# A fused mixer, MoE and two attention layers: split fills that run 8 chunks ahead, with their low parts kept in the weight ring

## The reference

```python
def even_layer(x, mem, ...):
    h = rms_norm(x, g) @ w_in
    y = concat([gdn_branch(...), diff_attention(dq, dk, dv, dg, ...), memory_attention(mq, mg, mem, ...)])
    return x + y @ w_out

def diff_attention(q, k, v, gate, ...):          # 8 heads, two softmaxes each
    q, k = rms_norm(q), rms_norm(k)
    p = softmax(q1 @ k1.T * scale + bias) - lam * softmax(q2 @ k2.T * scale + bias)
    return rms_norm(p @ v) * (1 - lambda_init) * silu(gate)

def odd_layer(x, mem, positions, ...):
    h = rms_norm(x, g) @ w_in                     # sq sk sv sg | mla q | c_kv | k_rope | mla gate | mq mg
    y = concat([window_attention(...), mla_attention(...), memory_attention(...)])
    return x + y @ w_out

def mla_attention(q, c_kv, k_rope, gate, positions, ...):
    k_nope, v = split(rms_norm(c_kv) @ w_kv_up)
    k = rms_norm(concat([k_nope, broadcast(k_rope)])); q = rms_norm(q)
    q, k = rope(q, positions), rope(k, positions)
    return softmax(q @ k.T * scale) @ v * silu(gate)
```

## Time and profile before

| | |
|---|---|
| median of 3 runs | 2868.59 us (2864.26 to 2870.82) |
| profiled execution | 2862.06 us, span 2860.3 us |
| mean granted clock of TensorE | 0.966 of full |
| PE busy | 2573.9 us, 90% of the span |
| DVE, ACT, POOL busy | 1334.4, 1087.0, 511.7 us |
| fill chunks | 288 (lows L798 x288, mean 1395 ns) |

### The profile page before, as it was taken

The page is one execution under the profiler, slowest core; times in us unless marked ns, Lnnn a source line. Parts: engine busy times, 40 slices in busy tenths (PEclk is TensorE's granted clock), DMA queues, the critical chain, the costliest instruction groups (busy, mean ns, idle before and its releaser), DMA issues. The chain is left out here.

```text
span 2860.3 us, 39591 instructions
## 1 busy us (share of the span) xinstructions
PE 2573.9 (90%) x14740; PEld 1873.2 (65%) x14740; DVE 1334.4 (47%) x2501; ACT 1087.0 (38%) x1922; POOL 511.7 (18%) x411
## 2 busy tenths in 40 slices
PE   8999999998888889999989999677889988978888
PEld 7984556886544444459957768565678767756667
DVE  5654784664211112347745545533435433474443
ACT  5553122443222122235434224344445344434444
POOL 0000110020011100010000000555530065064332
PEclk9999999999999999999999999898899989999999
DMA  7754344553599999945420135322244533432332
GB/s 300 220 205 152 134 145 144 184 199 123 239 422 422 422 421 422 380 187 179 172 81 32 46 126 197 119 103 103 103 148 150 177 114 115 147 118 104 130 116 107
DMA packets 80320, 529.77 MB, mean 185 GB/s; under 512 B 9088, under 2 KB 13568, under 8 KB 18848
## 3 DMA queue, kind: packets, MB, share of 16 engines
q1 hardware_dynamic: 76128, 514.50, 47.5%
q0 software_dynamic: 3456, 11.02, 1.5%
q10 hardware_dynamic: 576, 2.10, 0.2%
HBM read 520.24 MB, written 7.34 MB: 184 GB/s over the span
## 5 line engine op out<-in xcount | busy, mean ns | idle before, releaser
L798 POOL TENSOR_TENSOR parts_wl<-ring,parts_wh 128x512 fp32r<-128x512 f32 x288 | 396.3, 1395 | 1160.8 <-ACT parts_wh L783 1156.0
L759 PE MATMUL ps<-parts_wh,layer_xh 128*128 128x512 f32 x576 | 251.6, 437 | 107.8 <-POOL parts_wl L798 45.1
L2302 PE MATMUL ps<-ring,yT 128*64 128x256 f32 x2048 | 247.7, 386 | 52.6 <-DMA ring<-in_weights 48.5
L783 ACT ACTIVATE parts_wh<-ring 128x512 fp32r<-128x512 f32 x288 | 175.9, 629 | 276.9 <-PE ps L761 260.5
L760 PE MATMUL ps<-parts_wl,layer_xh 128*128 128x512 f32 x576 | 240.1, 417 | 0.0
L761 PE MATMUL ps<-parts_wh,layer_xl 128*128 128x512 f32 x576 | 239.6, 416 | 0.0
L2302 PEld LDWEIGHTS ps<-ring,yT 128*64 128x64 f32 x2048 | 137.7, 137 | 155.6 <-DMA ring<-in_weights 91.2
L1169 PE MATMUL ps<-ring,xT 128*128 128x512 f32 x512 | 222.0, 592 | 2.8 <-PEq L488 1.7
L759 PEld LDWEIGHTS ps<-parts_wh,layer_xh 128*128 128x128 f32 x576 | 117.3, 204 | 149.4 <-issue 58.6
L413 DVE TENSOR_TENSOR split_wl<-ring,split_wh 128x512 fp32r<-128x512 f32 x208 | 145.3, 709 | 96.5 <-ACT split_wh L387 95.4
L456 ACT ACTIVATE features_wh<-ring 128x512 fp32r<-128x512 f32 x208 | 130.3, 631 | 133.3 <-PE ps L473 133.3
(11 more groups left out here) (671 smaller groups left out, 5328.9 us busy)
## 6 DMA issues: line engine op xcount, KB each, us to landing
ring<-in_weights SPq DMA_DIRECT2D x468, 1024.0 KB, 5.0
x_res<-in_x SPq DMA_DIRECT2D x1, 2048.0 KB, 7.6
yT<-in_mem SPq DMA_DIRECT2D x1, 2048.0 KB, 15.7
rel_skew<-lru_feat POOLq DMA_DIRECT2D x1, 2048.0 KB, 49.8
mem_features<-yT ACTq DMA_DIRECT2D x4, 512.0 KB, 6.9
s_wb<-in_s_bc POOLq DMA_DIRECT2D x4, 512.0 KB, 3.9
s_wc<-in_s_bc POOLq DMA_DIRECT2D x4, 512.0 KB, 3.9
gate_bias<-in_gate_bias POOLq DMA_DIRECT2D x8, 256.0 KB, 3.9
```

What stands on the lines that cost most here:

```text
L759: mm(out, xh[:, kc, at], wh[:, c, :], start=kc == 0, stop=False)
L783: k.nc.scalar.activation(k.parts[0][:, c, :], k.ring[:, slot, c * BLK:(c + 1) * BLK], ACT.Copy).then_inc(w_high.sem, 1)
L798: k.nc.gpsimd.tensor_tensor(k.parts[1][:, c, :], k.ring[:, slot, c * BLK:(c + 1) * BLK], k.parts[0][:, c, :], ALU.subtract)\
L2302: last = nc.tensor.matmul(k.ps[s * WIN:(s + 1) * WIN, p, 0:FF], window[:, p, kc, :], k.ring[:, slot, at:at + FF], start=kc == 0, stop=kc = ...
```

## The change

- `LATE_DEEP = 8`: eight high buffers in place of four, and the lows lead by eight.
- The low part is written over the raw weights in the ring slot (`w_low` has the ring's address), so a slot is freed only by PE's last use of its low parts, in `gemm_tokens(late=True)` too.
- Steps are given out anew, so that blocks mostly end where a slot ends. In the attention, DVE stores an ended block after it has mixed the probabilities, not before.
- All four blocks of the latent input are fills of the window attention; the gate is cut into two blocks, one there, one in the MLA fill. The `gemm_tokens` at the start of `mla_branch` is gone.
- The rotary key's product is split like the others (`KeyProduct`): POOL makes high and low parts during the window gemm, and PE multiplies beside the norm of the latent.
- In `mla_rope`, ACT makes the two sines first and then the highs; evictions come once, at the end.

```diff
+LATE_DEEP = 8
...
-    CREDIT = SPLIT_DEEP
+    CREDIT = LATE_DEEP
...
 def gemm_tokens(...)
+        def high(j, kc):
+            return k.w_high[:, (j * chunks + kc) % deep, :] if late else wh[:, kc % deep, :]
+
+        def low(unit, turn, j, kc):
+            c = kc % UNIT_KC
+            return k.w_low[:, slot_of(unit, turn, 2 * upb), c * BLK:(c + 1) * BLK] if late else wl[:, kc % deep, :]
...
+                            if late and c == UNIT_KC - 1:
+                                mid.then_inc(k.unit_used, 1)
...
-                        dve.drain().then_inc(k.unit_used, 1)
+                        if not late:
+                            dve.drain().then_inc(k.unit_used, 1)
...
 class SplitFill:
-    LEAD = SPLIT_DEEP
+    LEAD = LATE_DEEP
...
-            act.wait_ge(w_used.sem, w_used.at(step - SPLIT_DEEP))
+            act.wait_ge(w_used.sem, w_used.at(step - self.LEAD))
...
+class KeyProduct:
+    def split(self, pool):
+        k, high = self.k, self.k.ev("small_high")
+        pool.wait_ge(k.loaded, k.loads)
+        k.nc.gpsimd.tensor_copy(self.high[:, :, :], self.raw).then_inc(high.sem, 1)
+        pool.wait_ge(high.sem, high.at(0))
+        k.nc.gpsimd.tensor_tensor(self.low[:, :, :], self.raw, self.high[:, :, :], ALU.subtract)
+    def multiply(self, pe, steps):
...
+            for kc in range(KC):
+                mm(out, xh[:, kc, at], self.high[:, kc, :], start=kc == 0, stop=False)
+                mm(out, xh[:, kc, at], self.low[:, kc, :], start=False, stop=False)
+                last = mm(out, xl[:, kc, at], self.high[:, kc, :], start=False, stop=kc == KC - 1)
...
 def attention(...)            # DVE
                     store(0)
                     if more:
                         begin(i + 1)
-                    store(1)
                     for j in pair:
...
                             dve.drain().then_inc(mixed.sem, 1)
-                    store(2)
+                    store(i, 1)
+                    store(i, 2)
...
-MEM_STEPS = {"evm": (8, (5, 5, 4, 2), 8), "odm": (6, (3, 3, 2, 2), 6)}
...
-              fill=fill, steps=first)
+              fill=fill, steps=8)
...
-              fill=fill, steps=steps)
+              fill=fill, steps=(3, 3, 1, 1))
...
-    head_norm(k, [v[:, t, 0:n].rearrange("p (h w) -> p h w", w=64) for v in (pq, pd) for t in range(NT)], 64, free, fill=fill, steps=8)
+    head_norm(k, [v[:, t, 0:n].rearrange("p (h w) -> p h w", w=64) for v in (pq, pd) for t in range(NT)], 64, free, fill=fill, steps=24)
...
-              fill=fill, steps=(5, 4, 4, 3), turned=free.rearrange("p (j a) -> p j a", j=2))
+              fill=fill, steps=[(4, 4, 4, 4)] * 3 + [(3, 3, 1, 1)], turned=free.rearrange("p (j a) -> p j a", j=2))
...
-              turn=Turned(k, lambda c, t: pq[:, t, c * P:(c + 1) * P], diff_x, HEADS, 7))
+              post=1.0 - lambda_init, gate=[pd[:, t, 2 * n:3 * n] for t in range(NT)], fill=fill, steps=16, early=8,
+              turn=Turned(k, lambda c, t: pq[:, t, c * P:(c + 1) * P], diff_x, HEADS, 14))
...
-        fill = SplitFill(k, (k.layer, KC, 2, tokens_to(k, mla_gate), None), (k.layer, KC, 2, tokens_to(k, pq), None))
+        fill = SplitFill(k, (k.layer, KC, 4, tokens_to(k, pq), None), (k.layer, KC, 1, tokens_to(k, mla_gate), None))
...
-        wait_loads(k, reach, bias, fill=fill, steps=4)
+        wait_loads(k, reach, bias, fill=fill, steps=8)
...
-        gemm_tokens(k, None, 2, KC // UNIT_KC, *store_tokens(k, pq, 2 * BLK), whole=k.layer, parts=k.parts)
...
-            rms_scale(k, ckv, ckv, n=KV_RANK, squares=squares)
+            rms_scale(k, ckv, ckv, n=KV_RANK, squares=squares, fill=product)
...
-            mla_rope(k, inner, pos, q_parts, kr, kv, rstd, free, fill, (8, 6))
+            mla_rope(k, inner, pos, q_parts, kr, kv, rstd, free, fill, 16)
...
+        k.w_high = nc.alloc_sbuf_tensor_at("late_wh", [P, LATE_DEEP, BLK], F32R, offset=xT_at)
+        k.w_low = nc.alloc_sbuf_tensor_at("late_wl", [P, LATE_RING, UNIT_KC * BLK], F32R, offset=ring_at)
```

More of the change, by code:

```diff
@@ L298, in first_pieces, with gemm_tokens @@
     return [slice(0, 1), slice(1, UNIT_KC)] + [slice(g, g + UNIT_KC) for g in range(UNIT_KC, chunks, UNIT_KC)]
-def gemm_tokens(k, x, blocks, upb, finish_act, finish_dve, dve_after_act=False, ahead=None, deep=SPLIT_DEEP, beside=None, after=None,
-                into=None, whole=None, parts=None, product=None):
+def gemm_tokens(k, x, blocks, upb, finish_act, finish_dve, dve_after_act=False, ahead=None, beside=None, after=None,
+                into=None, whole=None, late=False):
     nc, base = k.nc, k.used
@@ L386, in body @@
                             act.wait_ge(w_used.sem, w_used.at(j * chunks + kc - deep, turn, per))
-                            nc.scalar.activation(wh[:, c % deep, :], raw(unit, turn, c), ACT.Copy).then_inc(w_high.sem, 1)
+                            nc.scalar.activation(high(j, kc), raw(unit, turn, c), ACT.Copy).then_inc(w_high.sem, 1)
                         if g == 0 and not first:
@@ L412, in body @@
                             dve.wait_ge(w_high.sem, w_high.at(j * chunks + kc, turn, per))
-                            last = nc.vector.tensor_tensor(wl[:, c % deep, :], raw(unit, turn, c), wh[:, c % deep, :], ALU.subtract)
-                            last.then_inc(w_low.sem, 1)
-                        dve.drain().then_inc(k.unit_used, 1)
+                            nc.vector.tensor_tensor(low(unit, turn, j, kc), raw(unit, turn, c), high(j, kc), ALU.subtract).then_inc(w_low.sem, 1)
+                        if not late:
+                            dve.drain().then_inc(k.unit_used, 1)
                         if g == 0 and not first:
@@ L426, in gemm_tokens @@
     k.ended(evac_a=blocks, evac_v=blocks, x_high=len(pieces), x_low=len(pieces), w_high=steps, w_low=steps, w_used=steps)
-    if product is not None:
-        product.end()
 class FeatureSplit:
@@ L782, in make_highs @@
             slot, c = unit_wait(k, act, self.base + step // UNIT_KC, 0, 0), step % UNIT_KC
-            k.nc.scalar.activation(k.parts[0][:, c, :], k.ring[:, slot, c * BLK:(c + 1) * BLK], ACT.Copy).then_inc(w_high.sem, 1)
+            k.nc.scalar.activation(k.w_high[:, step % self.LEAD, :], k.ring[:, slot, c * BLK:(c + 1) * BLK], ACT.Copy).then_inc(w_high.sem, 1)
             self.high_at = step + 1
@@ L797, in lows @@
             pool.wait_ge(w_high.sem, w_high.at(step))
-            k.nc.gpsimd.tensor_tensor(k.parts[1][:, c, :], k.ring[:, slot, c * BLK:(c + 1) * BLK], k.parts[0][:, c, :], ALU.subtract)\
+            at = slice(c * BLK, (c + 1) * BLK)
+            k.nc.gpsimd.tensor_tensor(k.w_low[:, slot, at], k.ring[:, slot, at], k.w_high[:, step % self.LEAD, :], ALU.subtract)\
                 .then_inc(w_low.sem, 1)
@@ L2620, in end, with head_norm @@
         self.k.ended(turn_ready=1, tr=self.groups, **({"turn_high": self.groups} if isinstance(self.dst, tuple) else {}))
-def head_norm(k, parts, width, scratch, eps=EPS, mean=True, gain=None, post=1.0, gate=None, fill=None, steps=0, turn=None):
+def head_norm(k, parts, width, scratch, eps=EPS, mean=True, gain=None, post=1.0, gate=None, fill=None, steps=0, turn=None, early=0):
     nc = k.nc
@@ L2655, in _ @@
                     at += n
+                if early:
+                    fill.store_dve(dve, early)
                 if gain is not None:
@@ L2666, in _ @@
                     dve.drain().then_inc(k.ev("turn_ready").sem, 1)
-                    fill.store_dve(dve, turn.first)
+                    fill.store_dve(dve, turn.first - early)
                     turn.evict_dve(dve)
@@ L2670, in _ @@
                 elif fill:
-                    fill.store_dve(dve, steps)
+                    fill.store_dve(dve, steps - early)
             @block.gpsimd
@@ L2687, in _ @@
                     act.drain().then_inc(gated.sem, 1)
+                if early:
+                    fill.store_act(act, early)
                 if turn:
-                    fill.store_act(act, turn.first)
+                    fill.store_act(act, turn.first - early)
                     turn.evict_act(act)
@@ L2692, in _ @@
                 elif fill:
-                    fill.store_act(act, steps)
+                    fill.store_act(act, steps - early)
             @block.tensor
@@ L2809, in _ @@
                 if fill:
-                    fill.load(sp, turns * sum(steps))
+                    fill.load(sp, sum(sum(s) for s in by_turn))
             @block.gpsimd
@@ L2814, in _ @@
                 for i in range(turns if fill else 0):
-                    fill.lows(pool, sum(steps))
+                    fill.lows(pool, sum(by_turn[i]))
                     if beside is not None:
@@ L4139, in _ @@
             load(k, sp, pos[:, :], k.dram["positions"])
-            fill.load(sp, sum(steps))
+            fill.load(sp, steps)
         @block.tensor
         def _(pe):
-            fill.multiply(pe, sum(steps))
+            fill.multiply(pe, steps)
         @block.vector
@@ L4211, in _ @@
```

(2 more changed lines are left out.)

153 lines of the change are left out of this document (72 added, 81 removed).

## The result

The changed kernel takes 2838.98 us (median of 4 runs, 2836.61 to 2840.72) where the kernel before, on the same chip, takes 2866.43: a ratio of 0.9904, 95% interval 0.9885 to 0.9924. It is 27 us faster; 59 were forecast. Measured again later it stood at 0.9924 (0.9907 to 0.9941). The profiled execution took 2840.7 us, its span 2839.0.

What follows compares the result with a forecast made beforehand. TensorE was taken as the bound, at work 90% of the span, the end being its matmuls plus its holes. Stage terms summed to about -59 us on the profiled 2862.1: 2803, or 2810 in the runs; 8-in-10 range 2784 to 2848.

Steps and rivals of the forecast that it cites:

- Diff head norm: First stretch, 24 chunks instead of 8: 30.3 to 61 us, +31, with PE stalled about 12.6 us at chunk 17.
- both other head norms: Window head norm, 23.7 to 33.5 us (+9.8), and MLA head norm, 24.4 to 38.3 us (+13.9), each with 24 lows.
- Diff attention: Second stretch: 166.1 to 113 us, -53, with 56 chunks for 64 and 16-chunk turns of 29.3 us.
- needs 5.0: Diff attention turn: DVE's mixing takes 5.0 us from 1908.7, done at 1913.8, before PE arrives at 1914.7.
- Latent input: Latent stretch loses its 32 chunks and filler, keeps the norm, gets the key product: 54.4 to 14.7 us, -39.7.
- I take 11: Latent input: the key product's 96 matmuls of 64 columns take 11 us, from the old product's 0.113 us each.
- The estimate of 29 ns a matmul: Latent input: alternative of 2.8 us for the key product, about 7 us less in the sum; the prediction doubted it.
- Rope, MLA attention: Rope, attention and gate: 151.6 to 154 us, +2, with added chunks at +10.9 less waits.
- less the wait in rope (some 7): Rope, attention and gate: PE's wait of some 7 us in rope is subtracted from the added chunks' +10.9.
- Window rest: Sliding window after its head norm: 124.0 to 130 us, +6; chunks +16.4, less about 5 in each of two attentions.
- Rival A: Lead paid at barriers: five head norms at contended rate, diff turns stay 34 us through ACT's highs; 2848 to 2850; chance 0.18.
- rival C: Ring starves because PE's last use frees units later; slower, 2914 us at a landing of 15.4 us; chance 0.03.

Runs made afterwards that it cites:

- the wait for the mixing: Changed kernel, with POOL making no low part in a diff attention turn before DVE has mixed both softmaxes; 2835.9 us, 0.9892 to the kernel before.
- the first experiment: Changed kernel, with POOL's low part cut from 512 columns to 8 in every fill and PE reading the high part instead; 2764.5 us, one run.

## Why the prediction was wrong, by its steps

The direction, the order of the stages and most of their lengths held; the size did not: -59 forecast in the trace, -21 found.

- *Diff head norm* (stall 12.6 at chunk 17, block 61): right, 11.9 and 61.8. So were both other head norms, the subln, the memory attentions and the window gemm's end. Reckoning PE, ACT, DVE and POOL together, instruction by instruction, worked where it was done.
- *Diff attention* (-53, came as -30): the failed step is "needs 5.0". I took the mixing's length from a turn in which POOL made one low beside it, and put it at a time when POOL makes eight. It came to 10.8 us, and PE, which was to find it done, waited 4.31 us. The same prediction has DVE's scales at 2.29 us beside lows in the head norm, and leaves that out here. The Trainium skill's page that it cites ("SBUF — State Buffer", section "SBUF: two separate sides") has the lock held against either side. The trace agrees: six of the eight mixing operations take 1.33 to 1.60 us, about a low each, and POOL's eight lows 10.76 us in place of 10.3. Of the miss of 22.9 us the wait for the mixing took back 14 in its profile; 6 of the rest lie in its third turn. The opening and the last turn were not looked into.
- *Latent input* (-39.7, came as -32.8): "I take 11" was 18.3. The spacing of 0.112 was right while the clock was full. That the clock could fall under a run of narrow matmuls was in no row; the old product had kept it for 7.2 us. The estimate of 29 ns a matmul, worked out from the Trainium skill's "TensorE: Matmul & The Clock Gate" (section "Wait — 56ns, not 53.3ns?"), is not what the trace has: 112 ns at full clock and 214 at half, with a weight load for each matmul, and these loads busy all the while (4.00 of 4.00 us in the first of the two stretches above).
- *Rope, MLA attention* (+2, came as +9.7): "less the wait in rope (some 7)". The rope's length is DVE's chain, 32.5 us before and 33.9 after, and DVE's chain is again stretched by lows. The chunks added there were paid for in full. *Window rest* (+6, came as +10.6): the same subtraction, 5 us in each of two attentions, of which 5.8 came in all. That lows stretch DVE is not the reason here (0.9 us in the first experiment); what is was not tried.
- *The lead* was in no term by itself. Its cost at the barriers was in the head norms, its gain in the turns, and the gain fell with the mixing. Taken by itself, eight in place of four loses 12 to 18 us.

Rival A had the turn's length (34 us or more) and not its cause: it blamed ACT's highs, and the first experiment excludes them. Its sum, some 2849, lay nearer the measured time than the forecast did, but that is luck: 25 us of it are head norms at the contended rate, which came out as forecast. Of the hidden edits, the ring's longer hold cost nothing that shows (rival C): no high or low waits for a load in this half, and ring loads land in 4.9 us.

## What to carry to other kernels

A duration is good for the neighbours it was measured with: before moving an operation of DVE, look at what POOL does at the new time, and price both sides. More lead on an engine that must finish it at a barrier is a cost per barrier: 3.3 to 4.7 us at each head norm here, against 4.0 us gained in one attention and at most 1.6 in the others. A small product did best here laid out so that many columns move, and put where PE waits for another engine anyway.

## What the runs showed of the hardware

- POOL's subtractions and some of DVE's operations that only touch SBUF exclude each other almost whole, and with back-to-back lows DVE pays: a 0.42 us TENSOR_TENSOR takes 1.5, a SCALAR_TENSOR_TENSOR 1.33 to 1.60 in place of 0.44. TENSOR_SCALAR with one tensor in SBUF is hit as well (128x256: 0.35 us, 1.35 to 1.45 beside lows; 128x4: 0.17 or 4.12). DVE's SCALAR_TENSOR_TENSOR reading PSUM (685 ns) and its reductions in SBUF (1220 ns) are not.
- The granted clock fell from 1.00 to 0.50 during gapless split matmuls of 64 columns, after 21 to 49 of them (2.3 to 5.5 us), in every profile with that product except the one with wider matmuls between. Plain float32 ones of 64 columns, 64 records in 7.2 us, ran at 1.00 in the kernel before.
- Whether a hole costs clock differs between executions. After the same hole of 3.02 us, twelve equal matmuls ran at full clock in the changed kernel's profile and at half in that of the run that waits for the mixing (the first matmul behind the hole, then the stretch, for each):

```profile
2794.72 0.47 PE L764 MATMUL ps<-late_wh,layer_xh 128*128 128x512 f32 x1 [3.02 <-PEq L2827]
```

```profile
2794.70:2797.80 3.10, 3.00 (x12) 2.17 (x12) 1.29 (x2) 2.28 (x3) 0.00 (x0) 1.00 0.32 132
```

```profile
2792.39 0.77 PE L764 MATMUL ps<-late_wh,layer_xh 128*128 128x512 f32 x1 [3.02 <-PEq L2827]
```

```profile
2792.30:2797.60 5.30, 5.21 (x12) 4.02 (x13) 1.29 (x2) 2.33 (x3) 0.00 (x0) 0.50 0.20 83
```

  2.2 us for one hole. All thirteen profiles with the changed fills have this hole, 3.02 or 3.03 us long; the first matmul behind it took 0.47 us in nine of them and 0.76 or 0.77 in four. What decides it was not tried. It is reason enough to read edits worth a few us from their stages as well as from the total: four runs of the changed kernel beside each other lay 4 us apart, and six others 12.
